# The high part of the down weights' sums written a second time, to PSUM bank 7 in halves, and subtracted from there

## The reference

```
def swiglu(xn, p):
    return (jax.nn.silu(xn @ p['ffn_w_gate']) * (xn @ p['ffn_w_up'])) @ p['ffn_w_down']
```

## Time and profile before

| | |
|---|---|
| median of the runs | 3109.16 us |
| profiled execution | 3109.38 us |
| its span, first to last instruction | 3107.8 us |
| mean granted TensorE clock | 0.984 of full speed |
| TensorE busy | 2983.0 us (96%) |
| VectorE busy | 2166.2 us (70%) |
| ScalarE busy | 1345.7 us (43%) |
| GpSimd busy | 710.6 us (23%) |

### The profile page before, as it was taken

The page is one execution under the profiler, slowest core; times in us unless marked ns, Lnnn a source line. Parts: engine busy times, 40 slices in busy tenths (PEclk is TensorE's granted clock), DMA queues, the critical chain, the costliest instruction groups (busy, mean ns, idle before and its releaser), DMA issues.

```text
span 3107.8 us, 60002 instructions
## 1 busy us (share of the span) xinstructions
PE 2983.0 (96%) x23609; PEld 2862.4 (92%) x23609; DVE 2166.2 (70%) x2876; ACT 1345.7 (43%) x2037; POOL 710.6 (23%) x588
## 2 busy tenths in 40 slices
PE   8999999999999999999997999999999998998988
PEld 6789999998889999978797999999999998988988
DVE  4544336454665477565368999999999987788788
ACT  5442443334364555333355344343434444534344
POOL 0000000001353000010000122222211126678885
PEclk9999999999999999999998999999999999999999
DMA  7553223232216457886664444444444453424333
GB/s 275 181 179 110 81 77 95 88 95 71 69 42 218 160 194 245 287 317 237 236 203 136 131 126 128 127 132 125 121 129 126 126 186 116 167 88 154 102 106 144
DMA packets 457580, 460.56 MB, mean 148 GB/s; under 512 B 22619, under 2 KB 420988, under 8 KB 449551
## 3 DMA queue, kind: packets, MB, share of 16 engines
q1 hardware_dynamic: 436778, 357.88, 36.7%
q0 software_dynamic: 11712, 69.55, 5.9%
q10 hardware_dynamic: 8944, 31.12, 2.7%
HBM read 416.00 MB, written 42.74 MB: 148 GB/s over the span
## 4 chain that ended last, share of the span: by engine, by line
PE 78%; DVE 13%; ACT 3%; DMA 2%; issue 2%; POOL 1%; ACTq 0%; DVEq 0%; SPq 0%; POOLq 0%
PE ps L3180 16%; PE ps L3589 16%; PE ps L3786 12%; PE ps L3788 11%; PE ps L3787 11%; PE ps L3177 5%; DVE w_lo L3015 3%; DVE w_lo L3012 1%; DVE w_low L2033 1%; DVE set_low L3021 1%; ACT w_high L1215 1%; DMA w_raw<-in_xa_wo 1%; PE ps L3680 1%; DVE prods L2954 1%; DMA q_wide<-q_mid 1%
## 5 line engine op out<-in xcount | busy, mean ns | idle before, releaser
L3786 PE MATMUL ps<-set_high,w_hi 128*128 128x260 f32 x3584 | 1025.5, 286 | 56.4 <-DVE w_lo L3015 38.7
L3788 PE MATMUL ps<-set_high,w_lo 128*128 128x260 f32 x3584 | 1022.2, 285 | 0.0
L3787 PE MATMUL ps<-set_low,w_hi 128*128 128x260 f32 x3584 | 1022.1, 285 | 0.0
L2033 DVE TENSOR_TENSOR w_low<-w_raw,w_high 128x1024 fp32r<-128x1024 f32 x354 | 434.8, 1229 | 623.0 <-ACT w_high L1215 622.4
L3786 PEld LDWEIGHTS ps<-set_high,w_hi 128*128 128x128 f32 x3584 | 684.8, 191 | 64.2 <-DVE w_lo L3015 44.4
L3788 PEld LDWEIGHTS ps<-set_high,w_lo 128*128 128x128 f32 x3584 | 685.6, 191 | 0.0
L3787 PEld LDWEIGHTS ps<-set_low,w_hi 128*128 128x128 f32 x3584 | 684.0, 191 | 0.0
L1215 ACT ACTIVATE w_high<-w_raw 128x1024 fp32r<-128x1024 f32 x356 | 377.1, 1060 | 642.3 <-PE ps L3589 298.3
L1779 ACT ACTIVATE w_hi<-raw 128x768 fp32r<-128x768 f32 x168 | 142.4, 847 | 468.6 <-PE ps L3788 468.6
L3180 PE MATMUL ps<-x_high,w_high 128*128 128x260 f32 x1568 | 318.8, 285 | 2.6 <-DVE w_low L2033 2.4
L3180 PE MATMUL ps<-x_low,w_high 128*128 128x260 f32 x1568 | 314.5, 282 | 0.0
(11 more groups left out here) (560 smaller groups left out, 5375.6 us busy)
## 6 DMA issues: line engine op xcount, KB each, us to landing
w_raw<-in_w_in SPq DMA_DIRECT2D x96, 512.0 KB
raw<-in_ffn_w_up SPq DMA_DIRECT2D x176, 256.0 KB, 2.9
raw<-in_ffn_w_gate SPq DMA_DIRECT2D x176, 256.0 KB, 3.2
raw<-in_ffn_w_down SPq DMA_DIRECT2D x176, 256.0 KB, 3.0
w_raw<-in_w_out SPq DMA_DIRECT2D x64, 512.0 KB
w_raw<-in_xa_wq SPq DMA_DIRECT2D x64, 512.0 KB
w_raw<-in_xa_wo SPq DMA_DIRECT2D x64, 512.0 KB
set_raw<-h_mid ACTq DMA_DIRECT2D x22, 910.0 KB, 6.9
```

Of the source, the lines that this page charges most:

```text
L2033: dve.tensor_tensor(w_low[:, slot], w_raw[:, (g.slab0 + jj) % RAW], w_high[:, slot].bitcast(F32), ALU.subtract).then_inc(sem("w_low_ready" ...
L3786: pe.matmul(ps[:, bank, 0:HALF], high, set_high[:, kp, x], start=s + half == 0, stop=False)
L3787: pe.matmul(ps[:, bank, 0:HALF], high, set_low[:, kp, x], start=False, stop=False)
L3788: ins = pe.matmul(ps[:, bank, 0:HALF], low, set_high[:, kp, x], start=False, stop=s == len(tiles) - 1 and half == 1)
```

## The change

ScalarE writes the high part of a slab's sums twice: as before to `w_hi[:, 6:14]` for TensorE, and now also to PSUM bank 7 (`sum_high`, 512 columns), in two halves, since the bank holds 512 of the 1024. `high_sums(n, half)` does it: half 0 ahead of the plain blocks' high part, half 1 behind it. VectorE's `low_sums(n, half)` takes the low part from the sums in SBUF and the half in PSUM, in two instructions of 512 columns where there was one of 1024. Half 0 waits for `w_low` of the slab before; half 1 waits until VectorE has read half 0 (`sums_low`); VectorE waits for each half (`sums_high`), and for its second also for `w_hi`. At the start of the stage `down_low(UP + 1)` moves ahead of `set_low_down(0)`.

```diff
--- before.py
+++ after.py
@@ -106,14 +106,14 @@
...
-                       ("qs_rows", 4), ("k_t", NC // 2), ("s_exp", 1), ("os_rows", 1), ("s_o_high", 1), ("xa_root", 1), ("y_copied", Y_TILES)],
+                       ("qs_rows", 4), ("k_t", NC // 2), ("s_exp", 1), ("os_rows", 1), ("s_o_high", 1), ("xa_root", 1), ("sums_high", FF * D // 512), ("y_copied", Y_TILES)],
...
-                       ("s_probs", 1), ("s_spread", 1), ("s_o_low", 1), ("s_ssum", 1), ("xa_mean", 1), ("last_added", 2), ("y_first", 1), ("y_made", Y_TILES)],
+                       ("s_probs", 1), ("s_spread", 1), ("s_o_low", 1), ("s_ssum", 1), ("xa_mean", 1), ("sums_low", FF * D // 1024), ("last_added", 2), ("y_first", 1), ("y_made", Y_TILES)],
...
@@ -451,6 +451,7 @@
         q_mid = nc.dram_tensor("q_mid", (B, D), F32, kind="Internal").ap()
 
         ps = ctx.enter_context(nc.psum_tensor("ps", [P, 8, 512], F32))
+        sum_high = ps[:, 7].rearrange("p (b c) -> p b c", c=P).bitcast(F32R)
 
 
         def cols(w, it, j, blocks, col0, k0, kn, width=COLS):
@@ -1872,14 +1873,26 @@
             with act.Fori(PLAIN, FF - 1) as u:
                 up_unit(u)
 
+            def high_sums(n, half):
+
+                if half:
+                    act.wait_ge(sem("down_summed"), 3 * (n - UP) + 3)
+                    act.wait_ge(*after("sums_low", n - UP + 1))
+                else:
+                    act.wait_ge(sem("down_summed"), 3 * (n - UP) + 1)
+                    if n > UP:
+                        act.wait_ge(sem("w_low"), n)
+                act.activation(sum_high, sums_of(n)[:, 2 * half:2 * half + 2].rearrange("p s a c -> p (s a) c"), ACT.Copy).then_inc(sem("sums_high"), 1)
+
             def down_high(n):
 
                 k = n % 2
+                act.wait_ge(sem(f"raw_loaded{n % 4}"), 32 * (n // 4 + 1))
+                high_sums(n, 0)
                 act.wait_ge(sem("w_used"), n - (3 if n < UP + 2 else 1))
-                act.wait_ge(sem(f"raw_loaded{n % 4}"), 32 * (n // 4 + 1))
                 act.activation(w_hi[k][:, 0:6].rearrange("p (a b) c -> p a (b c)", a=2), raw[n % 4][:, :, 1:4].rearrange("p a b c -> p a (b c)"),
                                ACT.Copy).then_inc(sem("w_high"), 1)
-                act.wait_ge(sem("down_summed"), 3 * (n - UP) + 3)
+                high_sums(n, 1)
                 act.activation(w_hi[k][:, 6:14], sums_of(n)[:].rearrange("p s a c -> p (s a) c"), ACT.Copy).then_inc(sem("w_high"), 1)
 
             def set_load(kp):
@@ -3005,15 +3018,21 @@
                 for k in range(2):
                     up_unit(it * 2 + (1 + k), k, it * 16, it * 4)
 
+            def low_sums(n, half):
+
+                dve.wait_ge(*after("sums_high", 2 * (n - UP) + half + 1))
+                return dve.tensor_tensor(w_lo[n % 2][:, 6 + 4 * half:10 + 4 * half], sums_of(n)[:, 2 * half:2 * half + 2].rearrange("p s a c -> p (s a) c"),
+                                         sum_high.bitcast(F32), ALU.subtract)
+
             def down_low(n):
 
                 k = n % 2
                 dve.wait_ge(sem("w_high"), 2 * n + 1)
                 dve.tensor_tensor(w_lo[k][:, 0:6].rearrange("p (a b) c -> p a (b c)", a=2), raw[n % 4][:, :, 1:4].rearrange("p a b c -> p a (b c)"),
                                   w_hi[k][:, 0:6].bitcast(F32).rearrange("p (a b) c -> p a (b c)", a=2), ALU.subtract)
+                low_sums(n, 0).then_inc(sem("sums_low"), 1)
                 dve.wait_ge(sem("w_high"), 2 * n + 2)
-                dve.tensor_tensor(w_lo[k][:, 6:14], sums_of(n)[:].rearrange("p s a c -> p (s a) c"), w_hi[k][:, 6:14].bitcast(F32),
-                                  ALU.subtract).then_inc(sem("w_low"), 1)
+                low_sums(n, 1).then_inc(sem("w_low"), 1)
 
             def set_low_down(kp):
 
@@ -3058,8 +3077,8 @@
             slab_step(UP - 1, 3, ahead=False)
             hidden(FF - 2, 0, 16 * (FF // 2 - 1))
             down_low(UP)
+            down_low(UP + 1)
             set_low_down(0)
-            down_low(UP + 1)
             set_low_down(1)
             set_low_down(2)
             set_low_down(3)
```

## The result

The changed kernel takes 3190.01 us (median of four runs), the one before 3108.69 us beside it: a ratio of 1.0267 [1.0251, 1.0282], 81 us slower. The forecast was 3166 (3135 to 3200): the direction and the place are right, the size is short by 24 us. It lies above 3150 to 3180, the stretch that the prediction gave to its own mechanism (0.62), in the part of the range that was there for the clock.

A forecast was written before the change was run, and what follows sets the result against it. TensorE, at 96% of the 3107.8 us span, bounds the kernel. Parts one to four add 15.2, 5.3, 5.8 and 16, stage start and part changes 14: +56 on 3109.38 gives 3166 us (3135 to 3200).

The forecast's parts named there:

- The ring: Down stage: ScalarE and VectorE alternate over bank 7 without slack, 5.27 us a slab against TensorE's 5.0; chance 0.62.
- Half to PSUM, 0.60: Each added ScalarE write of 128x512 to bank 7 takes 0.60 us, 0.50 to the next start.
- Hand-over, 0.03: Passing work between ScalarE and VectorE costs 0.03 us each time, in either direction.
- There is no contention there to speak of: GpSimd's first sum is over when VectorE starts the plain blocks' low part, 1.41 us after the slab ahead ends.
- `down_sums` groups of GpSimd at 1.3 and 0.74: Sign of being right: GpSimd's sums in the down stage keep durations of 1.3 and 0.74 us.
- Second slab 6.80: A unit's second slab, with `combine` ahead of its low parts, ends 6.80 us after the first.
- Part four, 14.85: Two-slab units take 14.85 us against 12.19, with `square_out` delaying the next slab; +16 us over six units.
- Low of a half 0.69 whatever GpSimd does: Sign of being right: VectorE's 128x512 subtraction with one PSUM operand stays at 0.69 us, two costing 1.38 against 1.27.
- Changes of part: At the stage start and three part changes VectorE hardly pauses; a slab costs it 2.99 us; together +14 us.
- The relief: Parts two and three: the sums' low part no longer waits behind GpSimd's `add_out`, ending TensorE's 1.4 us wait a unit.
- The clock rival: TensorE's waits lower its granted clock in half the units, each losing about 2 us: +24, 3190 us; chance 0.12.
- Cheap halves: Rival: a half write takes 0.37 us, the ring 4.81, TensorE bounds again except behind `combine`; 3143 us; chance 0.14.

The follow-up runs named there:

- e5: Kernel before plus ScalarE's two writes of each half to bank 7, which nobody reads and which don't wait for VectorE; 3108.48 us, ratio 1.0002.
- e6: Kernel before with VectorE subtracting whatever bank 7 holds, in two halves, without ScalarE's added writes or any added wait; 3072.43 us, ratio 0.9891.
- e2: Changed kernel with ScalarE issuing the plain blocks' high part before half 0 and the sums' high part before half 1; 3111.16 us, ratio 1.0009.
- e7: Changed kernel with GpSimd's second sum of a slab waiting until VectorE has taken the low of half 0 of the slab ahead; 3174.84 us, ratio 1.0207.
- e10: Changed kernel; ScalarE writes the sums' high part before half 1, VectorE takes the plain blocks' low part between its two sums' lows; 3084.48 us, ratio 0.9927.
- e9: e10 with GpSimd's `add_out` also held until the low parts of the next unit's second slab are done; 3080.47 us, ratio 0.9913.

## Why the prediction was right, and short by 24 us

- **The ring and its place** (right, by experiment). e5 and e6 take the two halves of the change apart: the writes cost nothing, the reads save 34 us, so the waits between them cost an estimated 81 + 34 = 115, if the two add up (writes and reads together without the waits were not run). Half 0 starts 0.11 behind VectorE's last low (2613.24 + 0.69 to 2614.04), TensorE waits at every slab (0.25, 1.52 and 0.74 us in turn in part one; the prediction had 1.8 once in a unit and 0.3 at the others), and e2 gets all but 3 us back by order alone. What the prediction says of ScalarE's added work, that it would lie in its idle time and costs because of where it stands, holds.
- **Half to PSUM, 0.60** (right). It took 600 ns in 172 instances; the next starts 0.54 later (2614.04 to 2614.58), where 0.50 was set down.
- **Hand-over, 0.03** (mis-sized from VectorE to ScalarE). The row it came from is ScalarE to VectorE, and there it holds (sums high ends at 2620.09, the low starts at 2620.12). The other way it is 0.09 to 0.12 (0.11 and 0.09 in the unit shown), and the ring has two of these: 0.14 more a slab, and 0.08 with the two halves. That is the 5.47 against 5.27, and with no slack it stays in each slab. With the 0.08 of the second slab it is 0.5 in a unit of three, some 12 us in 24 units.
- **"There is no contention there to speak of"** (the step that failed). The sum took GpSimd's first sum alone to lie ahead of raw low. The second starts 0.01 ahead of raw low in the third slab and raw low ends 0.81 behind it: 6.06 in place of 5.47. e7 takes it away, with the collision of the second slab, and 15 us go. It is 0.59 in each unit of the window of part one and in 7 of the 12 of those of parts two and three, some 10 us in all. The sign "`down_sums` groups of GpSimd at 1.3 and 0.74" failed with it: where raw low goes first, the second sum takes 1.56.
- **Second slab 6.80** (6.88 measured), from `combine` and GpSimd's third sum as worked out: raw low ends at 2617.82, 0.81 behind that sum.
- **Part four, 14.85** (15.04 for one unit, then 15.7). `square_out` is in the ring as said: half 0 starts at 3103.63. But the wait ahead of raw low was put down to GpSimd's third sum (11.1 behind `combine`'s start); it is the first, which stands behind `add_square` and ends at 3106.04, 12.0 behind the `combine` at 3094.03: 0.9 a unit, and 4.4 us over the window's six units. ScalarE's `square_out` (first instruction) and half 0 there, VectorE's raw low, GpSimd's `add_square` and first sum:

```profile
3101.34 1.15 ACT L1934 ACTIVATE out_sq<-ffn_out 128x520 f32<-128x520 f32 x2
...
3103.63 0.58 ACT L1885 ACTIVATE ps<-down_sums 128x512 fp32r<-128x512 f32 x1
```

```profile
3105.01 1.84 DVE L3031 TENSOR_TENSOR w_lo<-raw,w_hi 128x768 fp32r<-128x768 f32 x1 [2.86 <-ACT w_hi L1893]
```

```profile
3102.03 2.76 POOL L1038 TENSOR_TENSOR out_ssum<-out_ssum,out_sq 128x520 f32<-128x520 f32 x2 [4.84 <-ACT out_sq L1934]
3104.75 1.29 POOL L1017 TENSOR_TENSOR down_sums<-raw 128x512 f32<-128x512 f32 x1
```

- **Low of a half 0.69 whatever GpSimd does** (right: 682 ns in the mean of 172, in all parts).
- **Changes of part** (+19.6 and the start +3.6, against 14 in all): short by 9. e7's trace has the three changes 7.1 us shorter than the changed kernel's (47.79, 49.17 and 34.98), so meetings with GpSimd can be most of it, though the collision of the second slab, which the prediction did count, is among them. How much the hand-overs, priced with the same 0.03, add there was not shown.
- **The relief** was in the sum for parts two and three, 1.4 a unit; e6 shows 1.4 to 1.5 there and 1.9 a unit in part four, which the prediction did not name. It makes no difference to the forecast, since the ring hid both, but it is what made a better version possible.
- **The clock rival** (wrong): the granted clock is 0.98, 1.00, 1.00 and 0.95 in the four windows, as before within 0.03, though TensorE now stands at every slab, 0.25 to 1.5 us in part one and 0.9 to 2.7 in part four. That this rival's number, 3190, is the measured one is chance: its mechanism isn't there, and its place in the range is what the measured time fell into.
- **Cheap halves** (wrong): 0.60. The Trainium skill (ScalarE: Activation LUTs, Step-by-step: what each stage is for) has ScalarE writing PSUM faster than SBUF, and the forecast's estimate was 0.55. In this trace raw high (768 columns) takes 831 and sums high (1024) 1042 ns, 211 for 256 columns; carried back to 512 columns that is an estimated 0.62 for a write to SBUF against 0.60 measured to PSUM. The sign agrees, as far as a line through two points can tell; the size is half of the some 40 ns by which the Trainium skill (Perfetto Trace Analysis, Optimizing Scalar/DVE Operations) has the access to PSUM cheaper. A 128x512 copy the other way, out of PSUM to SBUF, takes 596 ns in the same trace (L1915), some 20 less than 0.62 as well, so the 40 may be both ends together; no copy from PSUM to PSUM was run.

The rule on the contention, in the Trainium skill (SBUF — State Buffer, Who interferes with whom), is that VectorE with two SBUF inputs blocks wholly against GpSimd, and with one does not. All runs here agree: raw low ends 0.80 to 0.83 behind the end of the GpSimd instruction that was ahead of it, whether that had 0.4 us left or 2.2, and a low with its operand in PSUM took 0.67 to 0.69 in every one.

**Open:** the changed kernel's four runs spread over 8 us (3188.93 to 3196.91), and which units fall to 17.81 is decided by which engine gets ahead in a level start; that this is the cause of the spread was not shown. `down_low(UP + 1)` ahead of `set_low_down(0)` was in no run by itself. The spans up to the stage differ by 5 to 10 us between these executions, so a sum by stretches is good to a few us only.

## What to carry over

When a buffer is passed to and fro between two engines, write down the whole loop (both hand-overs, and everything that stands in either engine's list between the two ends) and hold it against the bound engine's time for the same work; an engine that is 45% busy is no cover if its instruction is the next link. Before dropping such a change, try the order in the lists: put what does not depend on the shared buffer (sums high, raw low) into the wait for it, which here turned 2.7% slower into 0.7% faster (e10), and 0.9% with `add_out` held (e9). Price the gain and the cost by themselves, with a kernel that reads without waiting and one that writes without being read.

## What the runs showed of the hardware

- From VectorE's end to ScalarE's start through a semaphore 0.09 to 0.12 us, from ScalarE's end to VectorE's start 0.03 to 0.04 (changed kernel, down stage).
- A 128x512 copy SBUF to PSUM (fp32r) on ScalarE takes 0.60 us, 0.54 to the next start. A 128x512 subtraction with one operand in PSUM takes 0.67 to 0.69 us on VectorE whatever GpSimd did in these runs.
- A 128x768 subtraction of two SBUF operands, 0.96 alone, ends 0.80 to 0.83 us behind the end of the GpSimd instruction ahead of it. Where the two start within 0.02 us of each other one of them pays: raw low 1.54 (GpSimd's sum 0.74), or the sum 1.56 (raw low 0.96); the starts as printed, to 0.01 us, don't always tell which.
- GpSimd's addition of 128x1040 (`add_out`) takes 2.44 us when it starts first, and 3.15 in the earlier trace rows, where raw low was already running and had 0.85 to go.
